# Two state-space steps per TensorE product, and sums of squares per token between two transformer blocks

## The chip, the cores and the metric

The kernel runs on one core of a Trainium2 chip. The metric is the device time of one execution in microseconds (us), as the median of several runs. The engines are TensorE (PE; its weight loads are shown as PEld), VectorE (DVE), ScalarE (ACT), GpSimd (POOL) and SyncE (SP), which issues most DMAs. Each runs its own instructions in order and waits for the others by semaphores.

## The reference

Two blocks run in sequence on 256 tokens of width 1024. Two parts of them matter here. In the first block a state-space mixer works on 512 channels in 32 groups, each with 64 complex states; between the blocks two norms follow each other.

```python
bu_re = jnp.einsum('blgh,gph->blgp', ug, bb_re)        # input products, bu_im likewise
...
_, _, s_re, s_im = lax.associative_scan(combine, (a_re, a_im, bu_re, bu_im), axis=1)
y = (jnp.einsum('blgp,ghp->blgh', s_re, c_re)
     - jnp.einsum('blgp,ghp->blgh', s_im, c_im)
     + d_skip * ug)                                     # output products and skip term
y = jax.nn.gelu(y.reshape(Bsz, L, SSM_WIDTH))
...
x = rms_norm(x, final_g)                                # end of the first block
...
h = rmsnorm(x, g_pre_mix[i]) * (1 + sc1) + sh1          # start of the second block
```

The second norm of a normed row needs only two sums per token, of x squared and of (x times final_g) squared, so both factors come from one pass over x. The second block's context rows are normed in the same place.

## The kernel before

**Order of the work.** Each engine has one function in the program, and its order is written out by hand. The stages are: modulation vectors and state-space matrices; the projections of the first block (loop over `IN1`, 12 chunks), with two chunks of modulation weights and one or two calls of `ssm_step` after each; the compression products of the attention (`hidR`, `hid`, `kc`); the first attention; merging; the first expert layer; the gap between the blocks; the projections of the second block, its attention and its expert layer. Weights come in chunks of 1 MB into a ring of 12 slots; SP waits for `freed`, which TensorE counts up when it is done with a slot.

**The state-space loop.** There are 16 steps j, each with two groups on 128 partitions of states. `ssm_in(j)` (line 699) makes the two input products (real and imaginary, n = 0, 1) from 32 rows of `uT` into bank 4 + j % 2 of PSUM. VectorE (lines 1960 to 1982) rotates them with sine and cosine tables (first reading the bank at lines 1969 and 1970, after which it counts `vemptied`), scans over the tokens, rotates back and writes the state to `ss2[j % 2]`. `ssm_out(j)` (line 711) multiplies the state into 32 rows of the outputs `y`, kept in banks 6 (steps 0 to 7) and 7 (steps 8 to 15). The rows `r` of a step are 32 * (j % 4). `ssm_step` calls `ssm_in` of one step and, from the third call on, `ssm_out` two steps behind. ScalarE makes the tables (`sines`, line 1536): for step j it waits for the state of step j - 2, and the copies of the projections out of PSUM stand in the same queue; TensorE's projections wait for the copy two before. After the last step VectorE adds the skip term in four instructions (line 1985), and "yD" releases the Gelu on ScalarE (line 1603) and the first attention on TensorE (line 966).

**Between the blocks.** After the first expert layer VectorE adds the residual in four parts (line 2331). ScalarE squares each part twice, plainly into `mgd` and with the final gain into `o2` (lines 1768 and 1770). TensorE sums both over the channels with a matrix of ones (line 1324), which leaves every sum in all 128 partitions, 256 tokens wide. VectorE forms the variances (lines 2337 to 2339), ScalarE takes the root, VectorE the reciprocal (line 2341), and then scales x into `hT` (line 2344); ScalarE adds the shift (line 1789), and TensorE begins the projections of the second block (`fill2`, line 1339). In the same stretch TensorE turns the context rows (`context_turn`) and ScalarE brings them out with gain and shift (`context_out`, line 1776). `occupy` issues products of zeros that keep TensorE busy; 24 of them stand here.

## Time and profile before

| what | us |
|---|---|
| runs shown, median (lowest to highest) | 2027.88 (2026.43 to 2030.33) |
| the profiled execution, its own time | 2024.26 |
| span of the profiled execution | 2022.5 |
| TensorE busy | 1828.0 |
| VectorE busy | 530.4 |
| ScalarE busy | 390.9 |
| DMA, mean rate over the span | 309 GB/s |

Times within the profile are counted from the start of the span. Busy times are sums over the whole span, in which the stages have different limits: in the first block and the front of the second TensorE works nearly without a pause, and in the expert layers the weights are awaited. An interval of interest is therefore read by its own rows. A float32 product shows as two records (two weight loads and two matmuls).

### The profile page before, as it was taken

Reading aid. Unit: us, or ns where it says so; the run is one execution under the profiler, and the core shown is the slowest. Engines: PE = TensorE matmul, PEld = TensorE weight load, DVE = VectorE, ACT = ScalarE, POOL = GpSimd, SP = SyncE. Lnnn points to the kernel's source line nnn. Section 1 sums busy time; section 2 is a strip of 40 time slices with the busy share of each in tenths; the row PEclk is TensorE's granted clock in tenths of the full one; section 3 lists DMA queues with packets and bytes.
Section 4 is the critical chain, followed back from the end, with each engine's and each line's share of the span. In section 5 each row is a group of like instructions: output and inputs, shape, how many; then the busy total and the mean of one; then the engine's idle time right before and its main releaser. Section 6 shows DMA issues by size and latency. Waiting matters only on the chain.

```text
span 2022.5 us, 28159 instructions
## 1 busy us (share of the span) xinstructions
PE 1828.0 (90%) x10814; PEld 995.4 (49%) x10829; DVE 530.4 (26%) x1218; ACT 390.9 (19%) x905; POOL 50.1 (2%) x109
## 2 busy tenths in 40 slices
PE   7999999987757899899999999988988999989987
PEld 4765777754534576678843333333333333333332
DVE  3676332131112132232432111111111111111112
ACT  4133452021101230343121110111110111100111
POOL 0040000000000010100010000000000000000000
PEclk9999999999988999999999999999999999999999
DMA  9968324519999661423456999999999899999997
GB/s 399 414 234 355 128 80 167 229 64 384 417 416 411 260 194 65 96 74 105 146 204 263 418 416 417 418 416 417 418 416 416 329 417 418 417 416 418 416 416 293
DMA packets 108633, 626.79 MB, mean 310 GB/s; under 512 B 11200, under 2 KB 15296, under 8 KB 50080
## 3 DMA queue, kind: packets, MB, share of 16 engines
q1 hardware_dynamic: 106688, 620.10, 76.1%
q0 software_dynamic: 1584, 4.33, 1.3%
q8 instruction: 71, 1.16, 0.2%
q10 hardware_dynamic: 272, 1.05, 0.1%
q14 instruction: 18, 0.15, 0.0%
HBM read 624.39 MB, written 1.05 MB: 309 GB/s over the span
## 4 chain that ended last, share of the span: by engine, by line
PE 58%; DMA 23%; SPq 11%; issue 3%; DVE 2%; ACT 2%; DVEq 1%; ACTq 0%
PE ps L467 56%; DMA ring<-in_w_gu_dram 15%; SPq L520 6%; DMA ring<-in_moe_w_gate_dram 4%; SPq L523 4%; PE ps L599 2%; DMA ring<-in_ada_w_dram 1%; DMA ring<-in_w_dn_dram 1%; DMA ring<-in_moe_w_down_dram 1%; ACT arena L1447 1%; SPq L493 0%; DVEq L1893 0%; PE ps L595 0%; PE ps L851 0%; SPq L423 0%
## 5 line engine op out<-in xcount | busy, mean ns | idle before, releaser
L467 PE MATMUL ps<-ring,arena 128*64 128x512 f32 (+2 forms) x5376 | 885.3, 546 | 125.0 <-issue 57.2
L467 PEld LDWEIGHTS ps<-ring,arena 128*64 128x64 f32 (+1 forms) x5376 | 289.3, 128 | 661.3 <-issue 475.2
L467 PE MATMUL ps<-arena 64*128 64x512 f32 (+11 forms) x1492 | 257.8, 410 | 25.7 <-ACT arena L1447 15.5
L467 PE MATMUL ps<-hT,ring 128*128 128x256 f32 (+1 forms) x960 | 236.4, 401 | 1.6 <-DVE hT L1910 0.8
L467 PEld LDWEIGHTS ps<-hT,ring 128*128 128x128 f32 x960 | 179.7, 191 | 56.4 <-issue 33.0
L467 PEld LDWEIGHTS ps<-arena 64*128 64x128 f32 (+7 forms) x1494 | 126.9, 156 | 142.7 <-issue 89.4
L2271 DVE TENSOR_SCALAR arena<-ps 128x512 f32<-128x512 f32 (+1 forms) x34 | 23.0, 676 | 532.7 <-PE ps L467 532.7
L1447 ACT ACTIVATE arena<-ps 128x512 f32<-128x512 f32 (+4 forms) x191 | 104.4, 570 | 271.5 <-PE ps L467 139.1
L1713 ACT ACTIVATE arena<-ps,mod,gain 128x128 f32<-128x128 f32 x176 | 66.2, 459 | 424.3 <-PE ps L467 424.3
L1725 ACT ACTIVATE arena<-arena 128x512 f32<-128x512 f32 (+1 forms) x44 | 25.3, 574 | 588.1 <-DVE arena L2271 391.2
L467 PEld LDWEIGHTS ps<-arena,hN 128*128 128x128 f32 x896 | 103.4, 192 | 32.2 <-issue 17.8
L467 PE MATMUL ps<-arena,hN 128*128 128x128 f32 x896 | 111.6, 280 | 2.4 <-DVE arena L2214 1.4
L467 PE MATMUL ps<-ring,hT 128*128 128x256 f32 (+2 forms) x416 | 80.9, 372 | 0.7 <-ACT hT L1789 0.6
L2258 DVE COPY arena<-ps 128x512 f32<-128x512 f32 x34 | 23.5, 692 | 214.1 <-PE ps L467 214.1
L599 PE MATMUL ps<-consts,arena 128*128 128x128 f32 x526 | 73.6, 276 | 5.7 <-DVE arena L2023 2.2
L467 PE MATMUL ps<-arena,ring 128*128 128x256 f32 x352 | 77.0, 380 | 0.7 <-ACT arena L1447 0.7
L467 PEld LDWEIGHTS ps<-ring,hT 128*128 128x128 f32 (+1 forms) x416 | 68.7, 182 | 13.6 <-issue 2.8
L599 PEld LDWEIGHTS ps<-consts,arena 128*128 128x128 f32 x526 | 60.2, 141 | 27.9 <-issue 14.4
L467 PEld LDWEIGHTS ps<-arena,ring 128*128 128x128 f32 x352 | 66.5, 190 | 11.9 <-issue 2.1
L1620 ACT ACTIVATE arena<-ps,stat 128x15 f32<-128x15 f32 (+3 forms) x128 | 56.1, 449 | 79.4 <-DVE stat L2006 79.4
L2006 DVE TENSOR_REDUCE stat<-ps 128x2 f32<-128x1024 f32 (+3 forms) x40 | 36.7, 917 | 120.8 <-PE ps L467 120.8
L467 PE MATMUL ps<-hN,ring 128*128 128x256 f32 x256 | 56.4, 380 | 0.0
(293 smaller groups left out, 914.5 us busy)
## 6 DMA issues: line engine op xcount, KB each, us to landing
ring<-in_w_gu_dram SPq DMA_DIRECT2D x256, 1024.0 KB, 20.3
ring<-in_w_dn_dram SPq DMA_DIRECT2D x128, 1024.0 KB, 23.2
ring<-dense_dram SPq DMA_DIRECT2D x56, 1024.0 KB, 9.2
ring<-in_moe_w_gate_dram SPq DMA_DIRECT2D x32, 1024.0 KB, 12.9
ring<-in_moe_w_up_dram SPq DMA_DIRECT2D x32, 1024.0 KB, 18.8
ring<-in_moe_w_down_dram SPq DMA_DIRECT2D x32, 1024.0 KB, 18.4
ring<-in_ada_w_dram SPq DMA_DIRECT2D x24, 1024.0 KB, 19.7
ring<-in_w_mod_dram SPq DMA_DIRECT2D x24, 1024.0 KB, 7.7
```

Source lines behind the costliest of these rows:

```text
L467: ins = nc.tensor.matmul(*a, start=start, stop=stop, **k)
L520: sp.dma_start(ring[:, i % RING, :], src).then_inc(full[i % RING], 16)
L523: sp.dma_start(slot_ap(i, (2, D)), src).then_inc(full[i % RING], 16)
L599: return nc.tensor.transpose(dst, src, ident[0:src.shape[0], 0:src.shape[0]])
L1447: return a(dst, src, ACT.Copy, scale=scale)
L1620: last = a(e_[:, s * nk:s * nk + m], ps[:, bank, at:at + m], ACT.Exp, bias=stat[:, i % 2, s:s + 1], accum_out=stat[:, i % 2, 4 + s:5 + s])
L1713: last = a(dst[:, d, :], ps[:, bank, k * P:(k + 1) * P], ACT.Identity, scale=gs[:, d:d + 1], bias=sh[:, d:d + 1])
L1725: a(sg[:, 0:w], glu[:, 0:w], ACT.Sigmoid, scale=1.702 if n == 2 else 1.0).then_inc(s["sig"], 1)
L2006: V.tensor_reduce(dst, sc[:, :, :, 0:m], AX.X, ALU.max, negate=True).then_inc(madeV, mark(madeV, ("mx", n, i)))
L2258: V.tensor_copy(dst, ps[:, 3, :]).then_inc(s["ys"], 1)
L2271: ts(glu[:, 0:w], ps[:, 1, 0:w], 7.0, None, ALU.min).then_inc(s["glu"], 1)
```

## The change

In the loop, `ssm_in(p)` makes the input products of steps 2p and 2p + 1 together, and `ssm_out(p)` the output products of both; within a call the two steps alternate, so that neighbouring instructions lie on different groups of 32 rows (inputs) or columns (outputs). The calls of `ssm_step` keep their places: even ones make inputs, odd ones from the fourth on outputs. The input banks follow a list, `bu_bank`, over banks 4, 5, 7 and later 4, 5, 6; bank 6 holds the first half of the outputs, so the skip term is added in two halves, the first after step 8, and the inputs of steps 10 and 11 wait for it. The states have a third buffer, made of constants that are no longer needed and of `rows`.

Between the blocks only the plain squares are made. They are now the stationary operand, and the moving one has two columns: ones, and the squared final gain (`sum_weights`). The sums come out per token on the partitions, two numbers for each of two blocks of 128 tokens; variance, root and reciprocal work on two to four columns. To spread the four columns over all partitions VectorE multiplies the identity with each (`diagonal`), and TensorE multiplies ones with that, into banks 6 and 7, from where VectorE reads the factors. 7 products of zeros remain of 24. ScalarE does part of the context columns before the root, part behind it, and the second block of tokens behind the shifts.

```diff
         sz = L(2, T)
-        ss2 = [L(2, T), L(2, T)]
+        ss2 = [[v[:, n, :] for n in range(2)] for v in (L(2, T), L(2, T))]
+        ss2.append([K[:, NCONST:NCONST + T], rows])
+        bu_bank = (4, 5, 7, 4, 5, 7, 4, 5, 7, 4, 5, 6, 4, 5, 6, 4)
         hid = L(TT, P)
...
         rn = sb("rn", [P, 24])
+        sum_weights = stat[:, :, :].rearrange("p a b -> p (a b)")[:, 0:2 * KD].rearrange("p (k n) -> p k n", n=2)
...
-            def ssm_in(j):
-                if j >= 2:
-                    pe.wait_ge(vemptied, nth(vemptied, ("bu", j - 2)))
-                elif j == 0:
+            def ssm_in(p):
+                if p == 0:
                     pe.wait_ge(emptied, nth(emptied, "cT"))
-                q, r = j // 4, 32 * (j % 4)
+                else:
+                    pe.wait_ge(vemptied, nth(vemptied, ("bu", 2 * p - 2)))
+                if p == 5:
+                    pe.wait_ge(madeV, nth(madeV, ("yD", 0)))
                 for n in range(2):
-                    last = mm(ps[:, 4 + j % 2, n * T:(n + 1) * T], bbT[r:r + 32, n, q, :], uT[r:r + 32, q, :],
-                              start=True, stop=True)
-                last.then_inc(filled, mark(filled, ("bu", j)))
-            def ssm_out(j):
-                pe.wait_ge(madeV, nth(madeV, ("s", j)))
-                q, r = j // 4, 32 * (j % 4)
+                    for j in (2 * p, 2 * p + 1):
+                        q, r = j // 4, 32 * (j % 4)
+                        last = mm(ps[:, bu_bank[j], n * T:(n + 1) * T], bbT[r:r + 32, n, q, :], uT[r:r + 32, q, :],
+                                  start=True, stop=True)
+                last.then_inc(filled, mark(filled, ("bu", p)))
+            def ssm_out(p):
+                pe.wait_ge(madeV, nth(madeV, ("s", 2 * p + 1)))
                 for n in range(2):
-                    last = mm(ps[r:r + 32, 6 + q // 2, (q % 2) * T:(q % 2 + 1) * T], cT[:, n, q, r:r + 32],
-                              ss2[j % 2][:, n, :], start=n == 0, stop=n == 1)
-                last.then_inc(filled, mark(filled, ("y", j)))
-            done_j = [0, 0]
+                    for j in (2 * p, 2 * p + 1):
+                        q, r = j // 4, 32 * (j % 4)
+                        last = mm(ps[r:r + 32, 6 + q // 2, (q % 2) * T:(q % 2 + 1) * T], cT[:, n, q, r:r + 32],
+                                  ss2[j % 3][n], start=n == 0, stop=n == 1)
+                last.then_inc(filled, mark(filled, ("y", p)))
+            ssm_steps = [0]
...
             def ssm_step():
-                if done_j[0] < 16:
-                    ssm_in(done_j[0])
-                    done_j[0] += 1
-                if done_j[0] >= 3 and done_j[1] < 16:
-                    ssm_out(done_j[1])
-                    done_j[1] += 1
+                i = ssm_steps[0]
+                ssm_steps[0] += 1
+                if i % 2 == 0 and i < 16:
+                    ssm_in(i // 2)
+                if i % 2 == 1 and 3 <= i < 18:
+                    ssm_out((i - 3) // 2)
...
             turn_modulation(4)
-            while done_j[1] < 16:
+            while ssm_steps[0] < 18:
                 ssm_step()
...
             pe.wait_ge(madeA, nth(madeA, "kc"))
-            pe.wait_ge(madeV, nth(madeV, "yD"))
+            pe.wait_ge(madeV, nth(madeV, ("yD", 1)))
             pe.wait_ge(emptied, nth(emptied, ("mod columns", 4)))
...
                 pe.wait_ge(madeA, nth(madeA, ("sq", "fin", c)))
+                if c == 0:
+                    pe.wait_ge(madeV, nth(madeV, "sum weights"))
                 for k in (2 * c, 2 * c + 1):
-                    for n, sq in enumerate((mgd, o2)):
-                        last = mm(ps[:, n, 0:T], ones, sq[:, k, :], start=k == 0, stop=k == KD - 1)
+                    for tt in range(TT):
+                        last = mm(ps[:, tt, 0:2], mgd[:, k, tt * P:(tt + 1) * P], sum_weights[:, k, :], start=k == 0, stop=k == KD - 1)
                 if c == 1:
...
             last.then_inc(filled, mark(filled, ("ss", "fin")))
-            occupy(7, 24)
+            occupy(7, 7)
+            for n, key in enumerate(("r12", "r1")):
+                pe.wait_ge(madeV, nth(madeV, ("diagonal", n)))
+                for tt in range(TT):
+                    j = 2 * n + tt
+                    last = mm(ps[:, 6 + n, tt * P:(tt + 1) * P], ones, rstd[:, j * P:(j + 1) * P], start=True, stop=True)
+                last.then_inc(filled, mark(filled, key))
...
                 sines()
-            act_.wait_ge(madeV, nth(madeV, "yD"))
+            act_.wait_ge(madeV, nth(madeV, ("yD", 1)))
             a(yS, yT, ACT.Gelu_apprx_tanh)
...
                 act_.wait_ge(madeV, nth(madeV, ("moe1 out", c)))
-                a(mgd[:, 2 * c:2 * c + 2, :], xT[:, 2 * c:2 * c + 2, :], ACT.Square)
-                for k in (2 * c, 2 * c + 1):
-                    last = a(o2[:, k, :], xT[:, k, :], ACT.Square, scale=cols[:, 0, 64 + k:65 + k])
-                last.then_inc(madeA, mark(madeA, ("sq", "fin", c)))
+                a(mgd[:, 2 * c:2 * c + 2, :], xT[:, 2 * c:2 * c + 2, :], ACT.Square).then_inc(madeA, mark(madeA, ("sq", "fin", c)))
...
             act_.wait_ge(filled, nth(filled, ("ctx", 0)))
-            context_out(0, 2, (0, 1, 4, 5, 6, 7))
-            sqrt("fin", rstd[:, 0:T])
+            context_out(0, 2, (0, 1, 4, 5))
+            sqrt("fin", rn[:, 8:12])
+            context_out(0, 2, (6, 7))
             act_.wait_ge(filled, nth(filled, ("ctx", 1)))
             context_out(0, 2, (2, 3))
-            context_out(1, 4, range(KD)).then_inc(madeA, mark(madeA, "hctx"))
             for c in range(4):
...
                 last.then_inc(madeA, mark(madeA, ("h2", c)))
-            sqrt("x2", rstd[:, T:2 * T])
+            context_out(1, 4, range(KD)).then_inc(madeA, mark(madeA, "hctx"))
             turn2 = [0]
...
+            def skip(half):
+                v.wait_ge(filled, nth(filled, ("y", 4 * half + 3)))
+                for k in (2 * half, 2 * half + 1):
+                    last = stt(yT[:, k, :], uT[:, k, :], cols[:, 2, 48 + k:49 + k], ps[:, 6 + half, (k % 2) * T:(k % 2 + 1) * T],
+                               ALU.mult, ALU.add)
+                last.then_inc(madeV, mark(madeV, ("yD", half)))
             fraction(0)
...
                     fraction(j + 2)
-                v.wait_ge(filled, nth(filled, ("bu", j)))
-                bu = ps[:, 4 + j % 2, :].rearrange("p (a b) -> p a b", a=2)
+                v.wait_ge(filled, nth(filled, ("bu", j // 2)))
+                bu = ps[:, bu_bank[j], :].rearrange("p (a b) -> p a b", a=2)
                 C, S_ = over(tb[:, 0, :], 2), over(tb[:, 1, :], 2)
...
                 step(tt_(sb_, sz, S_, ALU.mult))
-                if j >= 2:
-                    v.wait_ge(filled, nth(filled, ("y", j - 2)))
-                tt_(ss2[j % 2][:, 0, :], sa[:, 0, :], sb_[:, 1, :], ALU.subtract)
-                tt_(ss2[j % 2][:, 1, :], sa[:, 1, :], sb_[:, 0, :], ALU.add).then_inc(madeV, mark(madeV, ("s", j)))
-            v.wait_ge(filled, nth(filled, ("y", 15)))
-            for k in range(4):
-                last = stt(yT[:, k, :], uT[:, k, :], cols[:, 2, 48 + k:49 + k], ps[:, 6 + k // 2, (k % 2) * T:(k % 2 + 1) * T],
-                           ALU.mult, ALU.add)
-            last.then_inc(madeV, mark(madeV, "yD"))
+                if j >= 3:
+                    v.wait_ge(filled, nth(filled, ("y", (j - 3) // 2)))
+                tt_(ss2[j % 3][0], sa[:, 0, :], sb_[:, 1, :], ALU.subtract)
+                tt_(ss2[j % 3][1], sa[:, 1, :], sb_[:, 0, :], ALU.add).then_inc(madeV, mark(madeV, ("s", j)))
+                if j == 8:
+                    skip(0)
+            skip(1)
...
             V.reciprocal(rn[:, 4:6], rn[:, 4:6]).then_inc(madeV, mark(madeV, "ctx r"))
+            V.memset(sum_weights[:, :, 0], 1.0)
+            tt_(sum_weights[:, :, 1], cols[:, 0, 64:72], cols[:, 0, 64:72], ALU.mult).then_inc(madeV, mark(madeV, "sum weights"))
             v.wait_ge(filled, nth(filled, "moe1"))
...
             v.wait_ge(filled, nth(filled, ("ss", "fin")))
-            r12, r1 = rstd[:, 0:T], rstd[:, T:2 * T]
-            step(ts(r12, ps[:, 0, 0:T], EPS / D, EPS * EPS, ALU.mult, ALU.add))
-            stt(r12, ps[:, 1, 0:T], 1.0 / D, r12, ALU.mult, ALU.add).then_inc(madeV, mark(madeV, ("var", "fin")))
-            ts(r1, ps[:, 0, 0:T], 1.0 / D, EPS, ALU.mult, ALU.add).then_inc(madeV, mark(madeV, ("var", "x2")))
+            var12, var1 = rn[:, 8:10], rn[:, 10:12]
+            step(ts(var12, ps[:, 0:2, 0], EPS / D, EPS * EPS, ALU.mult, ALU.add))
+            ts(var1, ps[:, 0:2, 0], 1.0 / D, EPS, ALU.mult, ALU.add)
+            step(stt(var12, ps[:, 0:2, 1], 1.0 / D, var12, ALU.mult, ALU.add))
+            V.memset(crow[:, 3, 3:4], 0.0).then_inc(madeV, mark(madeV, ("var", "fin")))
             v.wait_ge(madeA, nth(madeA, ("std", "fin")))
-            step(V.reciprocal(r12, r12))
+            step(V.reciprocal(rn[:, 8:12], rn[:, 8:12]))
+            for n in range(2):
+                for j in (2 * n, 2 * n + 1):
+                    last = ts(rstd[:, j * P:(j + 1) * P], cst("ident"), rn[:, 8 + j:9 + j], None, ALU.mult)
+                last.then_inc(madeV, mark(madeV, ("diagonal", n)))
+            v.wait_ge(filled, nth(filled, "r12"))
+            r12, r1 = ps[:, 6, 0:T], ps[:, 7, 0:T]
             for c in range(4):
...
                 last.then_inc(madeV, mark(madeV, ("h2 scaled", c)))
-            v.wait_ge(madeA, nth(madeA, ("std", "x2")))
-            step(V.reciprocal(r1, r1))
+            v.wait_ge(filled, nth(filled, "r1"))
             for k in range(KD):
...

```

## Rows read from the trace of the kernel before

**Rows 1.** The chain that ended last, shares of the span by engine.

```profile
PE 58%; DMA 23%; SPq 11%; issue 3%; DVE 2%; ACT 2%; DVEq 1%; ACTq 0%
```

**Rows 2.** Stages: from:to, length, busy per engine (instructions), granted clock, DMA, GB/s.

```profile
50.60:172.30 121.70, 121.63 (x646) 82.17 (x642) 89.08 (x184) 30.90 (x70) 20.81 (x64) 1.00 0.84 325
705.60:725.80 20.20, 18.02 (x90) 13.34 (x91) 8.79 (x21) 14.51 (x34) 9.77 (x16) 1.00 1.02 309
725.80:1064.00 338.20, 325.62 (x1706) 239.98 (x1710) 111.44 (x182) 86.40 (x161) 18.42 (x24) 0.99 0.36 119
1064.00:2022.00 958.00, 871.89 (x4530) 324.37 (x4533) 165.06 (x423) 116.83 (x253) 0.00 (x0) 1.00 0.97 398
```

**Rows 3.** Timeline of VectorE, L1969: start, duration, instruction, idle time before it.

```profile
77.94 0.68 DVE L1969 TENSOR_TENSOR arena<-ps,arena 128x512 f32<-128x512 f32 x1
...
85.10 0.68 DVE L1969 TENSOR_TENSOR arena<-ps,arena 128x512 f32<-128x512 f32 x1
...
128.22 0.69 DVE L1969 TENSOR_TENSOR arena<-ps,arena 128x512 f32<-128x512 f32 x1 [1.26 <-PE ps L467]
...
139.21 0.69 DVE L1969 TENSOR_TENSOR arena<-ps,arena 128x512 f32<-128x512 f32 x1 [3.61 <-PE ps L467]
...
163.67 0.69 DVE L1969 TENSOR_TENSOR arena<-ps,arena 128x512 f32<-128x512 f32 x1 [2.51 <-PE ps L467]
...
183.93 0.69 DVE L1969 TENSOR_TENSOR arena<-ps,arena 128x512 f32<-128x512 f32 x1 [6.77 <-PE ps L467]
...
189.91 0.69 DVE L1969 TENSOR_TENSOR arena<-ps,arena 128x512 f32<-128x512 f32 x1
```

**Rows 4.** The chain that ended last, end of the loop: start, duration, engine, line.

```profile
172.28 8.98 PE ps L467 x80
...
195.66 1.06 PE ps L467 x4
...
198.44 1.06 ACT arena L1603
```

**Rows 5.** Timeline of all engines between the blocks, columns as in rows 3.

```profile
710.40 0.63 ACT L1768 ACTIVATE hN<-xT 128x512 f32<-128x512 f32 x1 [2.55 <-DVE xT L2331]
...
715.43 1.04 PE L599 MATMUL ps<-consts,hT 128*128 128x128 f32 x8
...
719.97 0.42 DVE L2337 TENSOR_SCALAR rstd<-ps 128x256 f32<-128x256 f32 x1 [7.24 <-PE ps L467]
...
721.25 3.59 ACT L1776 ACTIVATE hT<-ps,mod,gain 128x128 f32<-128x128 f32 x10
721.38 1.75 DVE L2341 RECIPROCAL rstd<-rstd 128x256 f32<-128x256 f32 x1
...
725.77 27.86 PE L467 MATMUL ps<-ring,hT 128*128 128x256 f32 x128 [0.62 <-ACT hT L1789]
```

**Rows 6.** Timeline of TensorE, one turn of the loop: state-space products, projection, products.

```profile
80.60 2.11 PE L467 MATMUL ps<-arena 32*128 32x256 f32 x8
82.64 7.17 PE L467 MATMUL ps<-hT,ring 128*128 128x256 f32 x32
...
91.59 2.11 PE L467 MATMUL ps<-arena 32*128 32x256 f32 x8
```

**Rows 7.** Timeline of TensorE, second attention: scores on 64 rows, then the next work.

```profile
879.29 1.13 PE L467 MATMUL ps<-arena 64*128 64x512 f32 x4
880.35 3.72 PE L467 MATMUL ps<-hT,ring 128*128 128x256 f32 x16
```

**Rows 8.** Timeline of TensorE, the gate projection with 48 moving columns.

```profile
164.55 3.77 PE L467 MATMUL ps<-ring,hT 128*128 128x48 f32 x32
```

**Rows 9.** Stretches with and without TensorE work, columns as in rows 2.

```profile
474.00:477.40 3.40, 0.00 (x0) 0.00 (x0) 0.00 (x0) 0.00 (x0) 0.00 (x0) 1.00 1.00 407
477.40:480.80 3.40, 3.29 (x32) 1.80 (x36) 0.00 (x0) 0.00 (x0) 0.00 (x0) 0.50 1.01 417
501.30:511.50 10.20, 2.56 (x25) 1.41 (x29) 0.00 (x0) 0.00 (x0) 0.00 (x0) 0.50 1.02 417
```

## Prediction

> **What bounds the kernel now.** I read the chain of waits by engine first [rows 1]: most of the span is TensorE work or weight transfers. Then the busy times by stage [rows 2]. While the state-space loop runs beside the projections (50.6 to 172.3 us) TensorE is busy for 121.63 of 121.7 us and VectorE for 89.08, so TensorE sets that stage, narrowly: a step on VectorE takes 7.16 us (77.94 to 85.10) when nothing holds it, and the rows that begin with a wait for TensorE (3.61 and 2.51 us) are steps that came to an empty bank [rows 3]. From 163.67 the end is set by step 12 on VectorE, ScalarE's sine tables behind it and the eviction of the gate projection, which lets TensorE go on at 172.28; then by steps 14 and 15, the last output product (195.66) and the skip products, after which attention starts at 198.44 [rows 4]. Between the blocks (705.6 to 725.8) the path is squares, sums, variance, root, reciprocal, scaling, shift [rows 5]: VectorE gets the sums at 719.97, and TensorE starts the projections at 725.77. From there to 1064 TensorE is 96% busy, and from 1064 on DMA is at 0.97 [rows 2]. The ring's loads are issued when TensorE frees a slot, so both later stages start earlier by whatever is won before them; I take all of it through to the end.
>
> **State-space products.** Today step j costs TensorE one input and one output product pair, 2.04 us in all (80.60 to 82.64), 1.02 each [rows 6]. The change puts the input products of two steps on two groups of 32 rows and of their outputs on two groups of 32 columns, in alternating order. The nearest row is two attention products of 512 columns on two groups of 64 rows: 1.06 us from start to start [rows 7]. Four products of 256 columns carry the same columns, so I take 1.06 for a paired input and for a paired output. Bounds: 0.9 (columns alone at the rate of the projections, 128 records of 256 columns in 27.86 us, is 0.87) and 2.04 (nothing shared).
> The new path, in legs; VectorE reads input j in its first product, and that start is what I follow:
> 1. Up to step 8 TensorE sets the pace. Ahead of input 8 stood nine input and six output products, 15.3 us; now five paired inputs and three paired outputs, 8.5. Step 8 on VectorE starts 6.8 us earlier, at 121.4 instead of 128.22 [rows 3].
> 2. After step 8 VectorE waits for the outputs of steps 6 and 7 to add the skip term, and step 9, whose input is already there, is queued behind that wait. TensorE reaches these outputs after a projection and two modulation chunks, 8.95 us [rows 6]: 121.3 + 8.95 + 1.06 = 131.3. Step 8 itself ends about 5.7 us after its start (as step 15 does: from 189.91 until its output begins at 195.66) [rows 3, 4], at 127.1: a new stall of 4.2 us. Two skip products take half of the 1.7 us between 196.72 and 198.44 [rows 4], 0.85. The usual 1.5 us follow before step 9 reads its input: 133.6 instead of 139.21, 5.6 earlier.
> 3. Steps 9 to 12 follow at 7.16 us; their inputs are ready (TensorE reaches input 12 at 132.2 + 1.06 + 9.5 + 1.06 + 8.95 + 1.06 = 153.8, with 0.55 for a turn of modulations in it). Step 12 starts at 155.1 instead of 163.67: 8.6 earlier, and so is TensorE's go at 172.28.
> 4. TensorE's work up to input 14 is unchanged, so step 14 starts at 175.3; step 15 needs no new input and starts 5.98 later (183.93 to 189.91) [rows 3]; it ends at 187.0, the paired output at 188.1, two skip products instead of four at 189.0. Attention starts 9.4 us earlier than at 198.44.
> TensorE gives up 16 us of products, but VectorE's own 7.16 us a step is late next. SP's queue gains from it: the loads wait for freed slots and are issued earlier with TensorE; DMA is at 0.84 in this stage [rows 2]. The third state buffer and the third bank cost nothing: they are other addresses. I take **-9.4 us**; at 0.9 a pair 1.3 more; unshared, by the same legs, step 9 at 142.4, step 12 at 165.7 and the skip at 201.5: +3.1.
>
> **Between the blocks.** ScalarE drops eight gained squares; the first square is done at 711.03 [rows 5]. TensorE's 16 sums of 256 columns become 16 products with two moving columns, 32 records. Nearest row: 32 records with the same stationary shape and 48 columns, 3.77 us [rows 8]. So 711.1 + 3.8 + 1.0 for the eight transposes between them [rows 5] puts the sums at 715.9 instead of 719.97. Upper bound: a record as dear as in the projections, 0.218, which gives 719.1; below 3.8 the squares' own pace (four of 0.63 us behind VectorE's residuals) leaves at most 1 us.
> Then, instead of 5.8 us (719.97 to 725.77): variance and root on two to four columns, bounded by the 1.41 us they take at 256 columns (719.97 to 721.38), 1.2 taken; reciprocal 0.2 instead of 1.75; two diagonal tiles, 0.6 (at most 0.42 each); two products with 128 columns, four records, 0.7 with their latency; two scalings 0.85; two shifts 0.85. In all 4.4: TensorE starts at 720.3, **-5.5 us**. ScalarE no longer has ten context columns ahead of the shifts (3.59 us) [rows 5]; the eight that moved behind them take 2.9 and end near 725.6, and TensorE needs them after the first 32 records, near 727.2: 1.6 us of cover. The weights of the sums are made before the expert block ends. The 24 filler products become 7; at full clock these end before the diagonals arrive.
>
> **The clock.** In both places TensorE now has less to do: about 3.3 us idle before the compression products (160.4 to 163.7) and over 5 us of narrow products and transposes between the blocks, where it was busy for 18.02 of 20.2 us at granted clock 1.00 [rows 2]. The trace shows what idling costs: after an idle 474.0 to 477.4 the granted clock was 0.50 (1.2 GHz) for 3.4 us while TensorE was busy for 3.29; in another place it was 0.50 for 10.2 us [rows 9]. I charge one short fall, half of 3.4: **+1.7 us**; bounds 0 and one long fall, 5.1, in each place.
> The Trainium skill ("TensorE: Matmul & The Clock Gate", Part 1) has the low clock as the resting state that work releases, which speaks against cutting the filler; the rows above agree.
>
> **Sum.** -9.4 - 5.5 + 1.7 = -13.2 us. The profiled execution took 2024.26 us (span 2022.5 and 1.8 around it), so 2011.1 on its scale; the median of the runs shown, 2027.88, lies 3.6 above it: 2014.7.
>
> **Rivals.**
> - *The tiles share less.* Each product keeps its own start, the 0.17 us by which 1.02 exceeds the 0.85 of its columns, so a pair takes 1.25 or more. Eight products up to step 8, the outputs ahead of step 9 and those at the end cost 0.19 more each, some 2 us: -11.2, 2016.7. 
> - *The change doesn't do what it says:* nothing is shared, the loop loses 3.1, and the gap keeps -5.5 and the clock's 1.7: -0.7, 2027.2. [rows 7] speaks against it.
> - *The narrow sums are as dear as wide ones* (0.218 a record): the gap gives only 2.3, the total is -10.0, 2017.9. [rows 8] speaks against it.
> - *Slower, by the clock.* Its place is the two gaps; its price is half a microsecond for each that TensorE then works at 0.50. It decides when more than 29.8 us of bound TensorE time (14.9 saved before the clock, doubled) run at 0.50: the projections after 720 and the compression products after 163.7 would each have to stay low longer than the 10.2 us of [rows 9]. At 32 us the time would be 2029; to be slower by over 0.2% takes 38 us, 2032.
>
> **How the numbers follow.** Forecast 0.58, tiles sharing less 0.16, dear sums 0.08, no sharing 0.12, slower by the clock 0.06. The no-sharing case lies within 0.2% (4.06 us, about what a measurement of this kernel tells from no change), and so does a clock case that stops short of 38 us, 0.02. Faster 0.82, same 0.14, slower 0.04. The predicted time is the forecast's, 2014.7. Low end: pairs at 0.9 (-1.3), no fall of the clock (-1.7), sums at the squares' pace (-1), and 2 us for how far the shown runs lie from their median: 2008.7. High end: less sharing, one long fall in each place (10.2 - 1.7) less what overlaps, and the same 2 us would pass 2025; the chance left above 2022.5 is about 0.15, so I stop there.
>
> **What would show it.** Right: paired inputs near 1.06 us; VectorE idle about 4 us after step 8 and back to back from step 9 to 13; attention at about 189; the second-block projections about 15 us before 725.77 in span time, as -9.4 and -5.5 add up. Wrong: paired products of 2 us; a wait of TensorE for the freed y bank longer than 1 us at step 10; granted clock 0.50 over the first projections of the second block; a DMA wait in the ring that was not there, which would mean that the gain is not passed on.

## The result, and the profile after

| | us | |
|---|---|---|
| kernel before, median of 3 (lowest to highest) | 2027.88 | 2026.43 to 2030.33 |
| changed kernel, median of 3 (lowest to highest) | 2014.91 | 2014.60 to 2015.52 |
| ratio, 95% interval | 0.994 | 0.9925 to 0.9955 |
| changed kernel again, on another occasion: 6 runs against 17 of before | 2015.32 against 2025.96 | ratio 0.9942, 0.9926 to 0.9958 |
| the two profiled executions, span | 2013.7 against 2022.5 | 8.8 less |

The change makes the kernel 0.6% faster: 13.0 us by the first medians, 10.6 us by the larger sets. The forecast was 2014.7 us. The time came out as forecast, but the profile doesn't show the terms of which the sum was made, and most of what follows is about that.

The stages of the changed kernel, cut where the loop's main part, the gap between the blocks, and the second expert loop begin and end (from:to, length, then busy time of TensorE, of its weight loads, VectorE, ScalarE, GpSimd, granted clock, DMA share, GB/s); they answer to [rows 2]:

```profile
50.60:164.30 113.70, 108.66 (x640) 76.78 (x641) 90.10 (x187) 30.75 (x69) 22.68 (x64) 1.00 0.90 353
704.00:718.84 14.84, 13.00 (x67) 10.74 (x65) 6.70 (x23) 6.58 (x16) 9.81 (x16) 0.65 1.03 301
...
1055.30:2013.00 957.70, 873.85 (x4533) 325.39 (x4533) 164.87 (x421) 116.86 (x253) 0.00 (x0) 0.99 0.97 398
```

In the loop TensorE gives up 13 us of work (121.63 to 108.66 busy) and the stage gets 8 us shorter; VectorE's work stays as it was. Between the blocks the granted clock is 0.65 on average where it was 1.00. In the last stage nothing changed but its beginning.

VectorE in the changed loop (start, duration, instruction, idle time before it and its releaser): L1989 is the first product that reads an input, L1974 the skip term. Below it, on TensorE, a paired output and a paired input, each with the work that follows it, and the paired input that waited for the skip term:

```profile
121.67 0.69 DVE L1989 TENSOR_TENSOR arena<-ps,arena 128x512 f32<-128x512 f32 x1 [0.64 <-PE ps L470]
131.49 0.87 DVE L1974 SCALAR_TENSOR_TENSOR arena<-arena,cols,ps 128x256 f32<-128x256 f32 x2 [3.93 <-PE ps L470]
133.85 0.68 DVE L1989 TENSOR_TENSOR arena<-ps,arena 128x512 f32<-128x512 f32 x1
...
155.70 0.69 DVE L1989 TENSOR_TENSOR arena<-ps,arena 128x512 f32<-128x512 f32 x1
...
177.66 0.69 DVE L1989 TENSOR_TENSOR arena<-ps,arena 128x512 f32<-128x512 f32 x1 [8.90 <-PE ps L470]
```
```profile
79.42 1.03 PE L470 MATMUL ps<-arena 128*32 128x256 f32 x8
80.38 7.17 PE L470 MATMUL ps<-hT,ring 128*128 128x256 f32 x32
...
120.49 1.13 PE L470 MATMUL ps<-arena 32*128 32x256 f32 x8
121.55 7.17 PE L470 MATMUL ps<-hT,ring 128*128 128x256 f32 x32
...
132.51 1.13 PE L470 MATMUL ps<-arena 32*128 32x256 f32 x8 [1.07 <-DVE arena L1974]
```

These answer to [rows 3] and [rows 6]. Eight records, four products, take 1.06 us from start to start as a paired input (120.49 to 121.55) and 0.96 as a paired output (79.42 to 80.38), where four records took 1.02. Then the loop's tail on TensorE, first before and then after, which answers to [rows 4], and the granted clock in one stretch of before and two of after:

```profile
172.28 7.13 PE L467 MATMUL ps<-ring,hT 128*64 128x256 f32 x64
...
198.50 1.72 PE L467 MATMUL ps<-arena 128*128 128x30 bf16 x20 [1.80 <-issue]
```
```profile
164.30 8.81 PE L470 MATMUL ps<-ring,hT 128*64 128x256 f32 x64 [3.97 <-ACT arena L1598]
...
189.38 0.64 PE L470 MATMUL ps<-consts,arena 128*32 128x256 f32 x1 [3.34 <-DVE arena L2002]
...
192.32 2.88 PE L470 MATMUL ps<-arena 128*128 128x30 bf16 x20 [1.02 <-issue]
```
```profile
200.90:211.10 10.20, 7.69 (x27) 5.69 (x28) 3.72 (x14) 4.51 (x25) 0.00 (x0) 0.50 1.01 419
```
```profile
188.80:205.90 17.10, 13.93 (x73) 9.69 (x74) 6.26 (x22) 7.07 (x27) 0.00 (x0) 0.50 1.00 413
164.30:173.10 8.80, 8.80 (x68) 5.37 (x72) 4.24 (x9) 4.15 (x6) 0.00 (x0) 0.81 0.55 229
```

The compression products come 8.0 us earlier but take 8.81 us instead of 7.13: TensorE had idled for 3.97 us and was then granted 1.2 GHz for a part of them. Around the second idle, 3.34 us, the clock is 0.50 for 17.1 us, where before it was low for 10.2; attention's 20 first products take 2.88 us instead of 1.72.

Between the blocks TensorE's rows answer to [rows 5]; the row of before is that with which its gap begins:

```profile
709.17 0.28 PE L467 MATMUL ps<-csil,consts 128*128 128x1 f32 x2
```
```profile
704.00 0.28 PE L470 MATMUL ps<-csil,consts 128*128 128x1 f32 x2
...
705.91 2.05 PE L470 MATMUL ps<-stat,hN 128*128 128x2 f32 x16 [0.70 <-ACT hN L1783]
707.82 1.95 PE L602 MATMUL ps<-consts,hT 128*128 128x128 f32 x8
709.56 3.41 PE L470 MATMUL ps<-stat,hN 128*128 128x2 f32 x16
712.84 3.15 PE L598 MATMUL ps<-consts 128*128 128x512 bf16 x7
...
718.84 3.48 PE L470 MATMUL ps<-ring,hT 128*128 128x256 f32 x15 [1.15 <-ACT hT L1801]
```

From 707.6 to 717.9 the clock is 0.50: the second eight transposes take 1.95 us instead of 1.04, the fillers take 0.43 us each and stand ahead of the diagonals' products, which so begin at 715.78. The gap is 14.84 us long (704.00 to 718.84) against 16.60 before (709.17 to 725.77).

**Where 8.8 us went.** Set against the trace of before: at attention's first products 6.2 us are won (198.50 to 192.32), at the end of the first expert block 5.2 (709.17 to 704.00), at the projections 6.9 (725.77 to 718.84), and at the second attention's scores 5.4 (879.29 in [rows 7], 873.94 after). And then 3.6 more come from a place that the change doesn't touch, the entry of the second expert loop. The rows of before and, below them, of after:

```profile
1030.68 0.62 PE L467 MATMUL ps<-arena 96*64 96x512 bf16 x4 [0.41 <-issue]
1031.13 1.02 PE L467 MATMUL ps<-ring,arena 128*64 128x512 f32 x2
1034.01 15.45 PE L467 MATMUL ps<-ring,arena 128*64 128x512 f32 x62 [1.85 <-issue]
1049.39 2.05 PE L467 MATMUL ps<-arena,hN 128*128 128x128 f32 x16
```
```profile
1025.38 0.62 PE L470 MATMUL ps<-arena 96*64 96x512 bf16 x4 [0.46 <-issue]
1025.84 14.72 PE L470 MATMUL ps<-ring,arena 128*64 128x512 f32 x64
1040.48 2.05 PE L470 MATMUL ps<-arena,hN 128*128 128x128 f32 x16
```

Before, TensorE stops for 1.85 us after two of the loop's first 64 records, with nothing to wait for that the trace shows ("issue"), and is granted 0.50 from 1033.8 to 1037.2. After, the 64 run through. The lead grows from 5.30 us (1030.68 to 1025.38) to 8.91 (1049.39 to 1040.48), and stays near that to the end (8.8).

The second profiled execution of the changed kernel (after_again) divides its gain otherwise: 3.3 us at the end of the first expert block (705.92), a gap of 13.74 us with the clock at 0.50 for 6.8 us, 6.1 us at the projections (719.66), and again 3.5 more at the entry of the second expert loop (6.1 to 9.6 us). So the shares of the stages hold to 1 or 2 us; that the entry of the second loop gives 3.5 us is the same in both.

### The profile page after: what moved, and what is told of

Read it like the earlier page. It is cut to its first block, busy times and chain, and to the rows that moved or that the text cites. A ratio compares the mean times of both kernels' runs of the same rounds, so it can differ in the third digit from the quotient of the medians.

```text
span 2013.7 us, 28154 instructions
## 1 busy us (share of the span) xinstructions
PE 1815.8 (90%) x10819; PEld 990.5 (49%) x10820; DVE 527.0 (26%) x1224; ACT 387.9 (19%) x896; POOL 52.0 (3%) x109
## 3 DMA queue, kind: packets, MB, share of 16 engines
q8 instruction: 72, 1.18, 0.2%
## 4 chain that ended last, share of the span: by engine, by line
PE 58%; DMA 23%; SPq 10%; issue 4%; DVE 3%; ACT 1%; DVEq 1%; ACTq 0%
PE ps L470 55%; DMA ring<-in_w_gu_dram 15%; SPq L523 6%; DMA ring<-in_moe_w_gate_dram 4%; SPq L526 4%; PE ps L602 2%; DMA ring<-in_w_dn_dram 1%; DMA ring<-in_ada_w_dram 1%; DMA ring<-in_moe_w_down_dram 1%; ACT arena L1462 1%; DVEq L1905 1%; PE ps L598 0%; SPq L496 0%; DVE arena L1997 0%; DVE arena L1995 0%
## 5 line engine op out<-in xcount | busy, mean ns | idle before, releaser
L470 PE MATMUL ps<-arena 64*128 64x512 f32 (+12 forms) x1474 | 246.0, 413 | 25.8 <-ACT arena L1462 15.5
L470 PEld LDWEIGHTS ps<-arena 64*128 64x128 f32 (+7 forms) x1474 | 121.5, 159 | 132.8 <-issue 82.9
```

The source lines that it names most:

```text
L470: ins = nc.tensor.matmul(*a, start=start, stop=stop, **k)
```

## Experiments

Theory 1: the legs of the sum are right, but the clock takes more than the 1.7 us charged. Theory 2, formed after the first four runs: how much TensorE code stands ahead of a loop decides whether the loop waits for its code, and part of the measured gain is that. All but before_long start from the changed kernel or are a part of it.

**The two parts alone.** loop_only has the edits of the state-space loop, gap_only those between the blocks.

> The state-space part alone: paired products and the skip in two halves, with the wide sums and 24 fillers of the kernel before between the blocks. Theory 1 (the sum of the prediction is right in its legs, but the clock's falls in the loop's tail take more than the 1.7 us charged): attention's first products at 192 us or so, as in the trace of after (192.3, 6.2 earlier than 198.50), and the whole run 5 to 6 us faster than before. Rival (the legs as predicted, the clock costs half a short fall): attention at 189 to 190 and the run 8.5 us faster. Second rival (the gain is lost in the DMA of the expert loop): attention as in theory 1, but the run within 2 us of before.

Measured: 2020.16 us, ratio 0.9969 (0.9956 to 0.9981), 5.6 us below the median of before (2025.80). Attention starts at 190.88, between theory 1 and the rival, because the first low stretch came earlier and hit less: it lay at 156.5 to 163.4, and the compression products took 7.13 us. The second is there as in the changed kernel, 17.0 us from 187.3. At the end of the first expert block 4.8 us of those 7.6 are left (704.41), and the stall of the second expert loop is there as before (1.95 us). The size is theory 1's, and it is also clear that where the low clock lies moves from execution to execution.

> The part between the blocks alone: narrow sums, diagonals, 7 fillers, with the state-space loop of before. [...] Rival (the prediction's term): 5.5 us faster, the low clock in the trace of after being an accident of when its clock looks.

Measured: 2021.53 us, ratio 0.9973 (0.9962 to 0.9985), 4.3 us below before. The granted clock in the gap:

```profile
713.10:723.30 10.20, 9.87 (x41) 8.07 (x41) 2.40 (x12) 3.62 (x10) 6.82 (x12) 0.50 1.02 255
```

The gap is 14.85 us long, 1.75 less than before, and 14.84 in the changed kernel: the low clock takes as much with the loop of before ahead of it, which is theory 1. But the run gained more than that, and its trace says where: at the second expert loop TensorE stalls for 0.34 us instead of 1.85 and no low clock follows, 3.4 us in all. The stall now stands after 11 of the loop's first 64 records, not after two:

```profile
1031.33 2.74 PE L468 MATMUL ps<-ring,arena 128*64 128x512 f32 x11
1034.41 11.80 PE L468 MATMUL ps<-ring,arena 128*64 128x512 f32 x53 [0.34 <-issue]
```

This is the first sign of theory 2. The two parts add up to 9.9 us, the whole measures 10.6.

**Does the order within a pair matter?** The edit, in both helpers:

```
-                for n in range(2):
-                    for j in (2 * p, 2 * p + 1):
+                for j in (2 * p, 2 * p + 1):
+                    for n in range(2):
```

> The changed kernel with the four products of a pair in the other order, both of one step before both of the other, so that neighbours stand in the same group of rows or columns. Theory (neighbours on different groups run side by side): a paired input or output takes about 2.0 us instead of 1.06; by the prediction's legs the loop then loses 3.1 us against before, so the run is 8 to 12 us slower than the changed kernel: 2023 to 2027. Rival (the products are paced by something else, such as the fetch of the moving columns, and the order has no effect): 1.06 us a pair and the run as the changed kernel, 2015.

Measured: 2015.47 us, ratio 0.9958 (0.9933 to 0.9983), the changed kernel's time. The theory falls and its rival holds in the time, though not in its reason. A paired output with the work behind it, and three of the eight records of the last paired output:

```profile
79.49 1.06 PE L470 MATMUL ps<-arena 128*32 128x256 f32 x8
80.48 7.17 PE L470 MATMUL ps<-hT,ring 128*128 128x256 f32 x32
```
```profile
189.57 0.64 PE L470 MATMUL ps<-consts,arena 128*32 128x256 f32 x1 [3.33 <-DVE arena L2002]
189.58 0.64 PE L470 MATMUL ps<-arena 128*32 128x256 f32 x1
...
190.43 0.63 PE L470 MATMUL ps<-rstd,arena 128*32 128x256 f32 x1
```

From start to start the paired output takes 0.99 us (0.96 in the changed kernel), a paired input 1.07 (1.06).

Step 14 reads the buffer in consts and rstd, step 15 the one in arena. The program gives consts, rstd, arena, arena; the trace starts arena 0.01 us behind consts and 0.85 us ahead of rstd. In these rows a product on another group doesn't wait for those issued ahead of it on the first one, and the sharing does not hang on the order.

**The gap at full clock.** Fillers where TensorE is idle: 4 ahead of the sums, 2 after each of three parts, 8 ahead of the diagonals, 7 behind them.

```
             context_turn(0, 2)
+            occupy(0, 4)
...
-            occupy(7, 7)
+                else:
+                    occupy(0, 2, True)
...
+            occupy(7, 8)
...
+            occupy(0, 7)
```

> The changed kernel with filler products put where TensorE is idle between the blocks: 4 ahead of the narrow sums, 2 after each of the first three parts of them, 8 ahead of the diagonals and 7 behind them. Theory 1 (the low clock took the gap's gain): granted clock 1.00 from 704 to the projections, the sums done at 709.2 instead of 713.0 in the changed kernel's time, projections 5 us earlier, the run 4 to 5 us faster than the changed kernel, 2010. Rival (the narrow products are slow by themselves, a start and a weight load each, and fillers stand in their way): sums still 2 us for 16 records, no gain or 1 us slower, 2015 to 2016.

Measured: 2018.63 us, ratio 0.9966 (0.9953 to 0.9979), slower than the changed kernel by 3 us, which neither side expected. The gap, then the second expert loop:

```profile
704.16:716.26 12.10, 11.90 (x83) 8.72 (x83) 6.95 (x23) 6.57 (x16) 9.85 (x16) 1.00 1.03 315
```
```profile
706.08 1.04 PE L470 MATMUL ps<-stat,hN 128*128 128x2 f32 x8
706.98 0.59 PE L598 MATMUL ps<-consts 128*128 128x512 bf16 x2
...
1025.93 1.06 PE L470 MATMUL ps<-arena 96*64 96x512 bf16 x4 [3.57 <-issue]
```

Theory 1 holds where it was made: with the clock at 1.00 the gap is 12.10 us, 2.7 less than in the changed kernel and 4.5 less than before; the narrow records take 0.9 us for eight, some 3.6 for the 32, where the prediction had 3.8. But at the second expert loop TensorE now stands for 3.57 us. What moved in that time, by the DMA queues of this kernel from 1022.4 to 1025.9 (queue, kind: packets, MB, share):

```profile
q8 instruction: 1, 0.02, 2.1%
q14 instruction: 1, 0.01, 1.1%
```

One packet of instructions of 16 KB and one of half that, and nothing else (over the whole changed kernel the 72 packets of q8 move 1.18 MB and the 18 of q14 0.15). TensorE seems to wait for its own code; for which engine a packet is the trace doesn't say, and the next runs test it. The Trainium skill ("Runtime: NRT & Kernel Launch", section Instruction fetch mechanics) says that code comes in blocks of 16 KiB, that the fetch runs ahead along the straight line, and that a taken branch out of what is held costs a fetch; the packet's size and the place, the entry of a loop, agree.

The stall doesn't explain the whole loss: of the 2.7 us by which this profiled execution ends later than the changed kernel's, 1.2 are there behind the loop's first products (1041.66 against 1040.48); the rest comes later, and its cause stays open.

**Does the amount of code decide?** late_fill adds 16 fillers 840 us ahead of that place, where TensorE idles anyway:

```
+                    if i == 17:
+                        occupy(7, 16, True)
                     ssm_out((i - 3) // 2)
```

> The changed kernel with 16 filler products more ahead of the last paired output, where TensorE waits 3.3 us for VectorE anyway (186.0 to 189.4). Theory 2 (TensorE's own code comes by DMA in chunks, and where a chunk's edge falls at the entry of the second expert loop decides whether TensorE stalls there: 1.85 us in the kernel before, none in the changed kernel, 3.57 us in gap_filled, which has 18 products more): the 16 products bring back a stall of 1.8 to 3.6 us in which nothing but code arrives, some 840 us behind the place of the edit, and the run is 1 to 3 us slower than the changed kernel, 2016 to 2018. Rival (the stall of gap_filled came from its gap, or by chance): no stall at the entry, the clock stays up at the first products of attention and the run is 1 to 2 us faster than the changed kernel, 2013.

Measured: 2030.38 us, ratio to before 1.002 (1.0006 to 1.0034), 15 us slower than the changed kernel. The stall at the second loop's entry is there as theory 2 said (3.54 us), but the larger cost is in the first expert loop, which theory 2 had not looked at. TensorE's waits for issue there (440 to 700 us: total, times, longest), changed kernel first, and two stops of one turn of the loop, likewise changed kernel first:

```profile
PE ps L470 <- issue: 57.2, 9, 12.4
```
```profile
PE ps L470 <- issue: 71.8, 9, 16.0
```
```profile
503.62 3.60 PE L470 MATMUL ps<-ring,arena 128*32 128x256 f32 x34 [11.54 <-issue]
508.85 5.38 PE L470 MATMUL ps<-ring,arena 128*32 128x256 f32 x94 [1.62 <-issue]
```
```profile
508.20 2.74 PE L470 MATMUL ps<-ring,arena 128*32 128x256 f32 x18 [15.56 <-issue]
513.68 8.06 PE L470 MATMUL ps<-ring,arena 128*32 128x256 f32 x110 [2.74 <-issue]
```

The two waits grow from 11.54 and 1.62 us to 15.56 and 2.74. The second of the two also moves: it stands after 34 of 128 products in the changed kernel and after 18 in late_fill, 16 products earlier, as many as were added ahead of it. In all other kernels profiled here, none of which changes the number of products ahead of this loop, it stands after 34. So this stop belongs to a place in TensorE's code, and 14.6 us more of waiting there come from 16 products of 0.21 us that stood in idle time (attention began at 192.27, as in the changed kernel). The weights' DMA ran on beside these waits, unlike at the second loop.

**The same filler time in fewer products.** before_long edits the kernel before in one line; a long filler is an f32 product of 512 columns and has two records:

```
-            occupy(7, 24)
+            occupy_long(7, 6)
```

> The kernel before with one edit: the 24 short fillers (bf16, 512 columns, 24 products) between the blocks are 6 long ones (f32, 512 columns, two products each, so 12) of the same 5.2 us. Theory 2 (how much TensorE code stands ahead of the second expert loop decides whether the loop's first products wait for their code): with 12 products less, fewer even than the changed kernel has 9 less, the stall of 1.85 us at 1034 and the short clock fall behind it are gone, nothing else moves, and the run is 3 to 3.5 us faster than before. Rival (the stall and the clock fall at 1034 belong to what the change did in its two places, or to chance): the same time as before, stall still there.

Measured: 2024.29 us against 2025.96, ratio 0.999 (0.9979 to 1.0). Its rows at the second loop:

```profile
1031.07 0.62 PE L467 MATMUL ps<-arena 96*64 96x512 bf16 x4 [0.41 <-issue]
1031.52 14.40 PE L467 MATMUL ps<-ring,arena 128*64 128x512 f32 x64
```

The gap is 16.60 us long, as before; the stall and the low clock behind it are gone, and the lead grows there by 3.9 us in this execution. In the medians only 1.7 of it shows (2.3 in the means), half of what was expected, and the interval touches 1. That the stall hangs on the code ahead is shown by this and the table below. Why the medians give less than the one execution stays open.

All profiled kernels, by TensorE's records ahead of the second expert loop (f32 products count two, bf16 fillers one), against those of the kernel before. The last column counts the loop's records that run ahead of the stall, the four in front of its 64 included:

| records | kernels | stall at the loop's entry, us | stands after |
|---|---|---|---|
| -12 | before_long | none | |
| -10 | best_short | 0.36 | 15 |
| -9 | changed kernel (twice), unshared, early_in, gap_only | none; 0.34 in gap_only | 15 |
| -2 | gap_long, best | 1.50, 1.36 | 7 |
| 0 | before, loop_only | 1.85, 1.95 | 6 |
| +7, +9 | late_fill, gap_filled | 3.54, 3.57 | 0 |

With more code ahead the stall stands earlier in the loop. TensorE goes on 2.8 to 3.6 us after the loop's first record in the four middle rows, and in the last row its wait at the entry is as long. So the earlier the stall stands, the longer it is, as if each time the same packet were awaited.

**The gap at full clock with less code.** Seven long fillers in the same places, instead of the seven short ones.

> The changed kernel with its 7 short fillers replaced by 7 long ones (f32, 512 or 256 columns), spread as in gap_filled: one ahead of the narrow sums, one after each of the first three parts, two ahead of the diagonals, one behind them. Nearly as much code as the changed kernel. Theory 2 (gap_filled did win its 2.6 us between the blocks and lost them again to the arrival of code at the second expert loop): granted clock 1.00 between the blocks, projections 2 to 3 us earlier against the end of the expert block than in the changed kernel, no stall at the loop's entry, the run 2 to 3 us faster than the changed kernel, 2012 to 2013. Rival (a gap without the low clock gives nothing because something later holds the end): projections earlier, but the run at 2015 to 2018 without a stall for code.

Measured: 2016.23 us (2012.60 to 2018.91), ratio 0.9946 (0.9929 to 0.9963). The gap is 12.25 us with the clock at 1.00, but I had counted a long filler as one record: it has two, and 1.50 us of stall came back. It is no faster than the changed kernel; the theory's 2012 to 2013 was missed.

**The idle ahead of the compression products, used.** One line:

```
+            ssm_step()
             pe.wait_ge(emptied, nth(emptied, ("p1", turn[0] - 1)))
```

> The changed kernel with the last paired input (steps 14 and 15) issued ahead of the compression products, where TensorE waits 4.0 us for ScalarE, instead of behind them. No product more or less. Theory (what the changed kernel leaves in the loop's tail is the wait of step 14 for its input, 8.9 us, and the clock): step 14 reads at 170 instead of 177.7, step 15 ends at 182, TensorE no longer waits before the last output, attention's first products at 188 to 189 instead of 192.3, the run 3 to 4 us faster, 2011 to 2012. Rival (the compressed keys, whose last eviction ends at 185.3, and the modulation columns at 186.3 are next and nearly as late, and the clock falls all the same): attention at 190 to 191, 1 to 2 us faster.

Measured: 2008.49 us, ratio 0.9906 (0.9888 to 0.9923), 6.8 us faster than the changed kernel, more than either side expected:

```profile
164.48 7.13 PE L470 MATMUL ps<-ring,hT 128*64 128x256 f32 x64 [1.22 <-ACT arena L1599]
...
185.48 1.72 PE L470 MATMUL ps<-arena 128*128 128x30 bf16 x20 [1.02 <-issue]
```

Step 14 reads at 169.01 instead of 177.66. The line also brings the outputs of steps 12 and 13 forward, and TensorE no longer waits for VectorE ahead of the last output. The clock is at 1.00 over the compression products and at attention's first ones (low for 10.2 us only from 188.6 on): 6.8 us are won at attention (192.32 to 185.48), as many as in the medians. In the profiled execution, the slowest of the five, 4.1 are left at the end (2009.6 against 2013.7); the clock was low for 10.2 us between 813 and 827 there, and for 3.4 in the changed kernel's.

**All together.** best has this, the outputs of steps 6 and 7 right behind input 8 (in ssm_step: `if i == 8: ssm_out(3)`), and the long fillers; best_short has 8 records less ahead of the second loop (two long fillers for ten short ones there, and no filler behind the third part of the sums).

> The changed kernel with three edits: the last paired input ahead of the compression products, the outputs of steps 6 and 7 right behind the input of steps 8 and 9 (so that the skip term of the first half does not wait for them), and the 7 long fillers between the blocks. Theory: the outputs' part takes VectorE's stall of 3.9 us away, but TensorE's input 12, at 152.8, is then what step 12 waits for, so only 1.8 us of it arrive at the compression products; with 3 to 4 for the early input and 2 to 3 for the gap, 7 to 9 us faster than the changed kernel: 2006 to 2008. Rival (the parts hide each other, or the code's arrival takes them back): 2010 to 2013.

> The kernel best with 8 filler products less ahead of the second expert loop: 10 short fillers ahead of the loop become 2 long ones (4 products), and the long filler behind the third part of the sums goes. Theory 2: the stall of 1.36 us at the loop's entry is gone; with it the run is 1.4 to 2 us faster than best, 2005.5 to 2006. Rival (fewer fillers ahead of the loop let the clock fall there, at half speed for its first products): as best or slower, 2007.5 to 2010.

Measured: best 2007.61 us, ratio 0.9909 (0.9891 to 0.9927), within what was expected: attention starts at 183.16, the gap is 12.26 us, and 1.36 us of stall took a part back. best_short 2004.71 us, ratio 0.9885 (0.9868 to 0.9903), the fastest: the stall is 0.36 us, the gap 12.01 us with the clock at 1.00. Its median is 2.9 us below that of best, which was measured on another occasion; each against its own runs of before, 2.5 are left, and the intervals overlap. In the two profiled executions the loop's entry is 1.0 us shorter and the end 0.6 earlier. The direction is theory 2's; the size is not shown.

> The changed kernel once more, with more runs of it and of the kernel before on one chip, for the size of the gain. Theory (the kernel before spreads over 10 us, its first three runs lay high in that spread, and the change is worth 10 to 11 us): 2015 us, 10 to 11 us below the median of before, TensorE's records at the entry of the second expert loop without a stall. Rival (13 us, as in the first comparison, is the size): 13 us below.

Measured: 2015.32 us (2014.10 to 2019.23) against 2025.96 (2024.17 to 2032.40): 10.6 us, the theory.

## Why the number held although its terms did not

- **Paired products, and legs 1 to 3: right.** A paired input takes 1.06 us, a paired output 0.96 (1.06 forecast for both). Step 8 read at 121.67 (121.4 forecast), the new stall behind it ended at 131.49 (131.3), step 9 read at 133.85 (133.6), step 12 at 155.70 (155.1), the compression products began at 164.30 (163.7). TensorE's wait at step 10, named as a sign of error above 1 us, was 1.07 and harmless: step 10 came after it anyway.
- **Leg 4: wrong by the clock.** Step 14 read at 177.66 (175.3), attention began at 192.32 (189). Of these 3.3 us 0.6 come from leg 3, 1.7 from the compression products at half speed, 0.9 from the last output at half speed. The low clock then lasted 17.1 us where before it lasted 10.2, and 1 us more was gone at the end of the expert block: 5.2 won of 9.4 in this execution.
- **The gap: its parts nearly right, its clock wrong.** 11.1 us were forecast; 12.10 were measured with the clock held at 1.00 (7.6 to the sums, 4.5 behind them), and 14.84 in the changed kernel. The sums came 9.0 us after the block's last product (6.7 forecast), the projections 5.8 after them (4.4). 1.8 won of 5.5.
- **The term that was mis-sized is the clock's: +1.7.** Both places fell, as the upper bound had it, and not one short fall in all. What the falls took is 2.7 us in the gap (14.84 against 12.10) and some 3.6 in the loop (9.4 forecast, 5.2 left, 0.6 of the rest from leg 3). The row behind the 1.7 was an idle of 3.4 us with a fall of 3.4; the row with 10.2 stood beside it [rows 9]. And the trace of before had a low stretch of 10.2 us at this very place, 200.90 to 211.10, which the prediction did not show. In the gap the clock fell at 707.6, after 0.7 us of idle and the first narrow products and transposes. That the long idle lets it fall is argued only: in after_again it was low already from 157.2 to 160.7, while TensorE was busy without a pause from 150.0 on.
- **Passing on: right but not whole.** 6.9 us at the projections, where the forecast's sign of being right was about 15, became 8.8 at the end. Some 1.6 were lost up to the second attention, in a stretch where the clock was 0.50 from 820.3 to 823.7, and 3.6 came at the second expert loop. No rival had that place; the sum had counted the 17 fewer fillers as time alone, not as code.
- **From the profiled execution to the median: wrong.** 3.6 us were added because the profiled execution lay under the median of three. Over 17 runs that median is 2025.96, and the offset 1.7.
- So -13.2 was forecast, about -10.6 is the size, and the profile has -6.9 in the two places, 1.6 lost and 3.6 won beside them. The error of the clock (some 4.6 us too little), the gift at the second loop (3.6) and a base of three runs that lay 1.9 us high made 2014.7 out of it. That the point was met is luck. The range would have held the time without it.
- The slower rival named the right mechanism, and its place. It needed 29.8 us of bound TensorE time at 0.50; the loop's tail and the gap had 30.8 us at 0.50 (3.4, 17.1 and 10.3), in which TensorE was bound for a part only.
- In the rival on less sharing, the 0.85 us of columns is 0.87 by the prediction's own row (128 records in 27.86 us), which changes nothing in it.

## What to carry to other kernels

Where a change takes work from TensorE, cost the clock in each place where it does, with the longest low stretch that the trace shows, above all at that very place (here 10.2 us, not 3.4). And look at once for work to pull into the idle: early_in moved a product there instead of a filler, with one line, and its median is 6.8 us lower. Count added and removed TensorE instructions as code as well as time: in front of a loop that waits for its code, 16 idle products cost 15 us in one kernel here, and fewer, longer fillers took a stall away. Such a wait shows as an "issue" row, and its place in the loop moves when products are added or removed ahead of it.

## What the runs showed of the hardware

- Products of 256 columns run side by side on two groups: four took 1.06 us on two groups of 32 rows and 0.96 on two groups of 32 columns, where two on one group took 1.02. The order in which they are issued made next to no difference (1.07 and 0.99 us in the other order), and a product on the second group started 0.85 us ahead of one issued before it on the first. The Trainium skill ("TensorE: Matmul & The Clock Gate", Part 3, the mechanism) has products in strict program order; the rows of the run with the other order show otherwise here.
- A product with two moving columns costs two records of some 0.11 us each at full clock (eight in 0.90 us, 706.08 to 706.98 in gap_filled) and 0.21 at half clock (sixteen in 3.28 us, 709.56 to 712.84 in the changed kernel).
- The stall for code at a loop's entry grew from nothing to 3.57 us over 21 records more of straight code ahead of it, and stood earlier in the loop the more there was; in another loop 16 records cost 14.6 us over its turns and moved one of its stops by 16 products.
- Where the low clock lies differs between executions of kernels that are alike up to there: the compression products took 8.81 us in the changed kernel and 7.13 us in loop_only.
